# The second layer's gate path moved into its projections, and two of its decay tables behind them

## The chip, the cores and the metric

The kernel runs on one core of one Trainium2 chip. The metric is the device time of one execution in microseconds, taken as the median of several runs. A core has TensorE (matmuls into eight banks of PSUM), VectorE, ScalarE, GpSimd and SyncE; here SyncE only issues DMAs. In the profile they are PE (PEld: its weight loads), DVE, ACT, POOL and SP.

## What is computed

Two networks stand one behind the other; the change is in the second one ("second block"), in the last of its two layers. A layer mixes 256 latent tokens and 256 context tokens of width 1024 and then applies an MLP. The mixer projects all tokens, runs two kinds of linear attention in both directions, and projects back. In the last layer the context is only read: it gives keys, values and gates but gets no output.

```python
def gla_log_gate(d, up, ub):
    return jax.nn.log_sigmoid((d @ up + ub).astype(jnp.float32)) / GLA_GATE_NORM

def hybrid_mixer(h, hc, w_in, ret_decay, gate_up, gate_b, gla_norm_g, row_pos, col_pos, need_ctx):
    lat = project_in(h, w_in)
    cx = project_in(hc, w_in)
    log_gamma = jnp.log1p(-jnp.exp(ret_decay.astype(jnp.float32)))
    ...
    r_lat, r_ctx = bidirectional_scan(retention_inputs(lat, True), retention_inputs(cx, False))
    g_lat, g_ctx = bidirectional_scan(gla_inputs(lat), gla_inputs(cx))
```

"Retention" has four heads of 128 with one constant decay for each head and direction. The "gated half" has four heads of 64 keys and 128 values, whose decay comes from the data: two rank-16 projections (`parts[8]`, `parts[9]`), a product with `gate_up`, a log-sigmoid, and a running sum over each chunk, from which exponentials are taken.

## The kernel before, in words

Matmuls that carry much weight are done as three products of high and low halves (`mm3`, L569): a value is split into a rounded high half and a remainder. The small ones of the attention are plain fp32. In the profile nearly all matmuls stand on L561, transposes on L576.

**Loads and splits.** SyncE streams weight chunks of 2 MB into a ring of four slots (`load`, L295). In the projections of the second block a chunk of 512 columns uses two numbers: the raw chunk lies in slot n, VectorE writes its high half into slot n+1 and its low half over the raw one (`split_chunk`, L2365: a cast on L2369, a subtraction on L2370). The ring therefore holds two such chunks. A load waits for `used`, a counter that TensorE raises with the first plain matmul after a chunk is done (`chunk_used`, L588, and `mm`, L560), or, where `flush` (L580) stands, with a drain.

**Projections of layer 1.** TensorE goes through chunks 0 to 6 in order and then a small eighth one with the 32 rank columns (the "rank tile"). A chunk has four tiles, taken round four banks (`tile_bank`, L592); ScalarE evicts each (`take`, L1398). Chunks 0 (retention queries), 3 and 6 (the output gates of the two halves) and the first two tiles of chunk 4 (gated queries) are needed for the latent tokens only, so they are 256 columns wide ("narrow"); chunks 1, 2, 5 (keys, values) and the rest of chunk 4 (gated keys) are 512 wide. Behind chunk 2 the rotations of queries and keys run (fp32, into banks 4 to 7), which VectorE applies behind its split of chunk 4. GpSimd computes the arguments of the decay tables of all four retention heads (`head_args`, L1892; lines 1896 to 1902), ScalarE their exponentials behind chunk 6 (`head_exps`, L1641). In layer 0 only heads 0 and 1 are done there and the other two in the attention, because their place is in use.

**Phase end.** `phase_end` (L538) is a barrier of four engines: each drains, raises `phase` and waits for all (PEq, ACTq or DVEq on L540 in the profile).

**Attention.** TensorE runs the four retention heads; for each head: a state product, scores, an intra product and an inter product, then two transposes for the next head. The eight matmuls of the gate products stand between the first scores and the first state. ScalarE copies transposed keys and states (`keys_out`, `state_out`), takes gates out with their bias (`gate_out`, L1696) and computes the log-sigmoid's logarithm in three steps (`gate_soft`, L1702). VectorE scales values and applies decay (`head_prep`, `head_decay`, `head_norm`), and for the gated half does a subtraction and two scans for a direction (`gate_sums`, L2473), then arguments, products, masks and states. Every engine's order is written out by hand; no scheduler reorders it. Behind it come the output projection and the MLP.

Of the kernel before, what the change touches and what calls it, by code (L numbers as in the profile page):

```python
# [19 lines left out]
F32 = mybir.dt.float32  # L20
F32R = mybir.dt.float32r
# [130 lines left out]
def build(nc, T, out):  # L152
    ctx = ExitStack()
    with ctx:
# [21 lines left out]
        mrow = [sb("mod_rows", [P, 512])[:, :], RS[:, :]]  # L176
        et = sb("chunk_decay", [P, 64])
        AR = 25600
        with ExitStack() as once:
# [6 lines left out]
            ar = shared("arena", [P, AR])  # L186

# [3 lines left out]
        ar_r = sb("arena_r", [P, AR], F32R)  # L191
        ps = [ctx.enter_context(nc.psum_tensor(f"bank{b}", [P, 512], F32))[:, :] for b in range(8)]
# [28 lines left out]
        MLP1 = L1 + 18  # L221
        END = MLP1 + 16
        WIN_ORDER = [1, 0, 3, 2, 4, 5, 6, 7, 8, 9, 10, 11]
# [70 lines left out]
        def _(sp):  # L294
# [60 lines left out]
            for l, first, mlp in ((0, L0, MLP0), (1, L1, MLP1)):  # L355
                for j in range(7):
                    load(first + 2 * j, cols(T["w_in_2"][l], j * 512, 512), as_cols(first + 2 * j))
                load(first + 14, cols(T["w_in_2"][l], 7 * 512, 2 * RANK), as_cols(first + 14, 2 * RANK))
                for j in range(2):
                    load(first + 16 + j, cols(T["w_out_2"][l], j * 512, 512), as_cols(first + 16 + j))  # L360
# [127 lines left out]
        first_w, second_w = [A3(22944, 2, L), A3(23456, 2, L)], [halves(mrow[0]), halves(RS[:, :])]  # L488
        third_w = [[A3(18848, 2, L), A3(19360, 2, L)], [X[:, 0:2, L:2 * L], X[:, 2:4, L:2 * L]]]
        fourth_w = [[A3(19872, 2, L), A3(20384, 2, L)], [X[:, 4:6, L:2 * L], X[:, 6:8, L:2 * L]]]  # L490
        WD_RQD = [[first_w, second_w, third_w[l], fourth_w[l]] for l in range(LAYERS)]
# [7 lines left out]
        GT1 = [H[:, 2 * d:2 * d + 2, :] for d in range(2)]  # L499
        GLg = [H[:, 4 + 2 * d:6 + 2 * d, :] for d in range(2)]  # L500
        GQM, GQD = GT1, GLg
# [54 lines left out]
        def _(pe):  # L556
# [491 lines left out]
            for l, first, mlp in ((0, L0, MLP0), (1, L1, MLP1)):  # L1048
                W = 2 * L if l == 0 else L
                for j in range(7):  # L1050
                    n = first + 2 * j
                    chunk_in(n + 1)
                    wh, wl = as_cols(n + 1, slot=low), as_cols(n, slot=low)
# [17 lines left out]
                    elif j in (2, 5):  # L1071
# [6 lines left out]
                    else:  # L1078
                        for nt in range(4):
                            wide = 2 * L if j == 1 or (j == 4 and nt >= 2) else W  # L1080
# [6 lines left out]
                    if j == 2:  # L1087
                        flush()
                        pe.wait_ge(S("b2_in"), 16 * (4 + 2 * l))
# [7 lines left out]
                n = first + 14  # L1097
                chunk_in(n + 1)
# [254 lines left out]
        def _(act):  # L1353
# [281 lines left out]
            for l in range(LAYERS):  # L1635
# [14 lines left out]
                for j in range(8):  # L1650
# [1063 lines left out]
```

## Time and profile before

| | us |
|---|---|
| median of three runs (1963.90, 1963.91, 1969.85) | 1963.91 |
| the profiled execution | 1969.83 |
| its span | 1968.0 |
| TensorE busy | 1866.7 (95%) |
| VectorE busy | 817.0 (42%) |
| ScalarE busy | 585.8 (30%) |
| GpSimd busy | 389.1 (20%) |
| mean granted clock of TensorE | 0.983 |

The busy times are for the whole span. Matmuls are pipelined, so TensorE's 95% doesn't say that each of its microseconds is needed. The granted clock is a share of 2.4 GHz. In the rows further down, a timeline row is start, length, engine, line, operation, outputs from inputs and their shapes; brackets give the idle time before it and who ended it. Several instructions in a row without a gap are merged (x16). A full fp32 matmul stands as two records.

### The profile page before, as it was taken

Reading aid. Unit: us, or ns where it says so; the run is one execution under the profiler, and the core shown is the slowest. Engines: PE = TensorE matmul, PEld = TensorE weight load, DVE = VectorE, ACT = ScalarE, POOL = GpSimd, SP = SyncE. Lnnn points to the kernel's source line nnn. Section 1 sums busy time; section 2 is a strip of 40 time slices with the busy share of each in tenths; the row PEclk is TensorE's granted clock in tenths of the full one; section 3 lists DMA queues with packets and bytes.
Section 4 is the critical chain, followed back from the end, with each engine's and each line's share of the span. In section 5 each row is a group of like instructions: output and inputs, shape, how many; then the busy total and the mean of one; then the engine's idle time right before and its main releaser. Section 6 shows DMA issues by size and latency. Waiting matters only on the chain.

```text
span 1968.0 us, 26165 instructions
## 1 busy us (share of the span) xinstructions
PE 1866.7 (95%) x11248; PEld 1367.2 (69%) x11248; DVE 817.0 (42%) x1342; ACT 585.8 (30%) x892; POOL 389.1 (20%) x205
## 2 busy tenths in 40 slices
PE   5999999999998989989999899999999899889998
PEld 2777796964443443436887657888888688679998
DVE  1615244731110111115342844556665625574333
ACT  2513103331111111114112535222333411544554
POOL 2000000120000000006002131443343250025665
PEclk9999999989999999999999999999999899999999
DMA  9469917569999999992223104345444232414451
GB/s 357 154 255 347 339 44 278 199 257 420 427 427 427 428 427 428 426 417 91 95 86 123 41 33 154 140 177 187 156 150 150 87 113 102 174 51 164 173 197 38
DMA packets 111425, 429.84 MB, mean 218 GB/s; under 512 B 5706, under 2 KB 8821, under 8 KB 98512
## 3 DMA queue, kind: packets, MB, share of 16 engines
q1 hardware_dynamic: 109056, 416.56, 54.5%
q0 software_dynamic: 2256, 11.62, 1.6%
q8 instruction: 90, 1.47, 0.3%
q14 instruction: 23, 0.19, 0.0%
HBM read 427.11 MB, written 1.05 MB: 218 GB/s over the span
## 4 chain that ended last, share of the span: by engine, by line
PE 66%; DMA 17%; DVE 5%; PEld 5%; ACT 3%; issue 3%; PEldq 1%; SPq 0%; POOL 0%; POOLq 0%; ACTq 0%; DVEq 0%
PE bank L561 65%; DMA ring<-in_moe_w_down 7%; PEld bank L561 4%; DMA H<-in_moe_w_down 4%; DMA arena<-in_moe_w_down 4%; DMA ring<-in_ada_w 2%; PE bank L576 1%; PEldq L540 0%; DVE H L1985 0%; DMA ring<-in_w_in 0%; DVE arena L2508 0%; DVE H_low L1992 0%; DVE ring_low L2584 0%; DVE ring_low L2165 0%; DVE ring_low L2578 0%
## 5 line engine op out<-in xcount | busy, mean ns | idle before, releaser
L561 PE MATMUL bank<-arena_r 128*128 128x256 f32 (+1 forms) x2176 | 591.1, 339 | 12.4 <-ACT arena_r L1385 6.5
L561 PE MATMUL bank<-arena_r,ring_low 128*128 128x512 f32 (+2 forms) x1920 | 596.0, 342 | 1.5 <-DVE H_low L1992 1.0
L561 PEld LDWEIGHTS bank<-arena_r 128*128 128x128 f32 x2176 | 384.5, 190 | 63.6 <-issue 18.8
L561 PE MATMUL bank<-arena 128*128 128x64 bf16 (+8 forms) x2892 | 362.4, 318 | 40.4 <-DMA arena<-in_hy_filt_w 11.7
L561 PEld LDWEIGHTS bank<-arena_r,ring_low 128*128 128x128 f32 (+1 forms) x1920 | 352.3, 188 | 47.4 <-issue 2.5
L561 PEld LDWEIGHTS bank<-arena 128*128 128x128 bf16 (+4 forms) x2892 | 203.8, 131 | 200.1 <-issue 172.4
L561 PE MATMUL bank<-H_low,arena_r 128*128 128x512 f32 (+1 forms) x672 | 216.5, 339 | 0.0
L561 PE MATMUL bank<-ring,arena 128*64 128x512 f32 x768 | 170.3, 598 | 10.0 <-DMA ring<-in_moe_w_down 9.5
L2566 DVE SCALAR_TENSOR_TENSOR X<-bank,mod,X 128x256 f32<-128x256 f32 x216 | 94.2, 478 | 196.6 <-PE bank L561 196.6
L1924 POOL TENSOR_TENSOR ring_low<-ring,arena_r 128x2048 fp32r<-128x2048 f32 x31 | 142.4, 4615 | 130.5 <-DVE ring_low L2578 68.6
L1399 ACT ACTIVATE arena<-bank 128x512 f32<-128x512 f32 (+2 forms) x106 | 51.2, 496 | 366.3 <-PE bank L561 366.2
L2338 DVE SCALAR_TENSOR_TENSOR arena_r<-bank,arena,arena_r 128x512 fp32r<-128x512 f32 x32 | 24.0, 750 | 308.8 <-ACT arena_r L1582 308.8
L1940 POOL TENSOR_TENSOR arena_r<-arena,arena_r 128x512 fp32r<-128x512 f32 (+1 forms) x64 | 104.5, 1646 | 222.9 <-ACT arena L1802 222.9
L561 PEld LDWEIGHTS bank<-ring,arena 128*64 128x64 f32 x768 | 56.7, 138 | 116.4 <-issue 116.1
L561 PEld LDWEIGHTS bank<-H_low,arena_r 128*128 128x128 f32 x672 | 125.0, 191 | 14.4
L2634 DVE SCALAR_TENSOR_TENSOR arena<-ring,arena 128x1024 f32<-128x1024 f32 x84 | 99.5, 1222 | 66.1 <-POOL arena_r L1940 62.6
L561 PE MATMUL bank<-H,arena 128*64 128x512 f32 (+4 forms) x464 | 116.3, 433 | 6.7 <-DVE arena L2508 2.5
L561 PE MATMUL bank<-X,ring 128*128 128x256 f32 x512 | 118.1, 386 | 0.0
L561 PEld LDWEIGHTS bank<-X,ring 128*128 128x128 f32 x512 | 96.5, 192 | 17.8 <-issue 4.7
L1795 ACT ACTIVATE arena_r<-ring 128x4096 fp32r<-128x4096 f32 x15 | 54.5, 3630 | 172.8 <-DMA ring<-in_w_mlp 123.8
L561 PE MATMUL bank<-H_low,ring_low 128*128 128x512 f32 (+2 forms) x272 | 93.4, 358 | 0.0
L561 PE MATMUL bank<-ring_low,arena_r 128*128 128x512 f32 x288 | 92.8, 394 | 0.0
(326 smaller groups left out, 1854.0 us busy)
## 6 DMA issues: line engine op xcount, KB each, us to landing
ring<-in_w_mlp SPq DMA_DIRECT2D x32, 2048.0 KB, 7.9
ring<-in_w_in SPq DMA_DIRECT2D x26, 2048.0 KB, 8.9
ring<-in_ada_w SPq DMA_DIRECT2D x24, 2048.0 KB, 11.7
ring<-in_moe_w_up SPq DMA_DIRECT2D x17, 2048.0 KB, 23.0
ring<-in_moe_w_gate SPq DMA_DIRECT2D x17, 2048.0 KB, 27.5
arena<-in_moe_w_up SPq DMA_DIRECT2D x15, 2048.0 KB, 22.7
ring<-in_moe_w_down SPq DMA_DIRECT2D x14, 2048.0 KB, 23.4
arena<-in_moe_w_down SPq DMA_DIRECT2D x13, 2048.0 KB, 24.2
```

Source lines behind the costliest of these rows:

```text
L561: ins = nc.tensor.matmul(o, l, r, start=start, stop=stop, skip_group_check=True)
L576: ins = nc.tensor.transpose(o, i, ident)
L1399: A_(o, i, f, **kw).then_inc(S("tile_free"), 1)
L1795: A_(W2h, slot(n), ACT.Copy).then_inc(S("w_high"), 1)
L1924: G.tensor_tensor(low(n)[:, s], slot(n)[:, s], W1h[:, s].bitcast(F32), ALU.subtract).then_inc(S("w1_split"), 1)
L1940: G.tensor_tensor(HAl[:, nt, 0:W], HA[:, nt, 0:W], HAh[:, nt, 0:W].bitcast(F32), ALU.subtract)\
L2338: V.scalar_tensor_tensor(YSl[:, s], ps[6 + nb][:, :], WSL, YSh[:, s].bitcast(F32), ALU.mult, ALU.subtract)\
L2566: i = V.scalar_tensor_tensor(X[:, t, s * L:(s + 1) * L], o[:, s * L:(s + 1) * L], mod[:, 1 + l, gate + t, s:s + 1], X[:, t, s * L:(s + 1) ...
L2634: d = V.scalar_tensor_tensor(CPROD[:, c, :], as_turned(n)[:, q % 3, :], 1.0, CSIL[:, c, :], ALU.mult, ALU.mult, accum_out=mod[:, 2, bass.d ...
```

## The change

In layer 1 alone:

- The chunks come in the order 0, 1, 2, 3, 6, 4, 5 (`IN_ORDER`). The eighth chunk is gone; `w_out` and the MLP's chunks move up by two numbers.
- The 32 rank columns come by a DMA of GpSimd into `mod_rows` (`TINY`), issued behind that of the gate weights, ahead of the end of layer 0's MLP. VectorE splits them ahead of chunk 2. TensorE does the rank tile right behind the rotations, ahead of chunk 3.
- The gate products stand ahead of the tiles of the sixth chunk in order (chunk 4), into banks 4 to 7. ScalarE takes them out and computes the first direction's logarithm behind chunk 6, the second one's ahead of the last chunk's tiles. VectorE does the first direction's running sums behind the last split, the second's behind the arguments of the column decays, the last thing ahead of the phase end; each as four scans of 256 in place of two of 512.
- The buffers of gates and logarithms move to places free in layer 1 (parts of `YT`, `RQ` and `X`). The decay tables of heads 2 and 3 take the places that they have in layer 0, and so are computed behind the phase end; head 1's table moves to `X`.

In layer 0 only views are written differently. Two semaphores are merged into one (`small_exp`).

```diff
@@ loads
+        IN_ORDER = ((0, 1, 2, 3, 4, 5, 6), (0, 1, 2, 3, 6, 4, 5))
+        OUT_AT = (16, 14)
-                for j in range(7):
-                    load(first + 2 * j, cols(T["w_in_2"][l], j * 512, 512), as_cols(first + 2 * j))
-                load(first + 14, cols(T["w_in_2"][l], 7 * 512, 2 * RANK), as_cols(first + 14, 2 * RANK))
+                for j, c in enumerate(IN_ORDER[l]):
+                    load(first + 2 * j, cols(T["w_in_2"][l], c * 512, 512), as_cols(first + 2 * j))
+                if l == 0:
+                    load(first + 14, cols(T["w_in_2"][l], 7 * 512, 2 * RANK), as_cols(first + 14, 2 * RANK))
@@ places
-        third_w = [[A3(18848, 2, L), A3(19360, 2, L)], [X[:, 0:2, L:2 * L], X[:, 2:4, L:2 * L]]]
-        fourth_w = [[A3(19872, 2, L), A3(20384, 2, L)], [X[:, 4:6, L:2 * L], X[:, 6:8, L:2 * L]]]
+        first_w, third_w, fourth_w = [[A3(o, 2, L), A3(o + 512, 2, L)] for o in (22944, 18848, 19872)]
+        second_w = [[halves(mrow[0]), halves(RS[:, :])], [X[:, 0:2, L:2 * L], X[:, 2:4, L:2 * L]]]
@@ TensorE, projections
+                def gate_mms(banks):
+                    for d in range(2):
+                        for t in range(2):
+                            mm(ps[banks[2 * d + t]], GUP[0:32, d, t * P:(t + 1) * P], DT[0:32, :], inc="gate_mm")
+                for j, chunk in enumerate(IN_ORDER[l]):
                     n = first + 2 * j
                     chunk_in(n + 1)
+                    if l and j == 5:
+                        pe.wait_ge(S("tile_free"), gates_tile + 1)
+                        gate_mms((4, 5, 6, 7))
...
+                        if l:
+                            pe.wait_ge(S("ranks_split"), 1)
+                            gates_tile = tiles[0]
+                            ranks_tile(*[t.rearrange("p (k n) -> p k n", k=KT) for t in (TINYh, TINY_r)])
@@ ScalarE
-                for j in range(8):
+                for j in (0, 1, 2, 3, 4, 5, 6, 7) if l == 0 else (0, 1, 2, 7, 3, 6, 4, 5):
+                    if l and j == 5:
+                        gate_soft(1)
...
                     if j == 6:
                         tables()
-                        for h in range(2 + 2 * l):
+                        for h in range(2):
                             head_exps(h)
+                        if l:
+                            for d in range(2):
+                                gate_out(d)
+                            gate_soft(0)
...
                 head_square(0)
-                if l == 0:
-                    head_exps(2)
+                head_exps(2)
                 state_out(1)
@@ GpSimd
                 if l:
+                    pool.wait_ge(S("ada_turned"), 8)
+                    bring(TINY.rearrange("p (k n) -> p k n", k=KT), cols(T["w_in_2"][l], 7 * 512, 2 * RANK), "b2_in")
                     phase_end(pool, "l0_mlp")
...
-                for h in range(1, 2 + 2 * l):
-                    head_args(h)
+                head_args(1)
                 phase_end(pool, f"l{l}_in")
-                for h in range(2 + 2 * l, RT_H):
+                for h in range(2, RT_H):
                     head_args(h)
@@ VectorE
+                if l:
+                    dve.wait_ge(S("b2_in"), 16 * (4 + 3 * l))
+                    link(V.tensor_copy(TINYh, TINY))
+                    V.tensor_tensor(TINY_r, TINY, TINYh.bitcast(F32), ALU.subtract).then_inc(S("ranks_split"), 1)
                 for j in range(1 + l, 5):
                     split_chunk(first + 2 * j)
...
+                if l:
+                    gate_sums(0)
...
                 i.then_inc(S("col_arg"), 1)
+                if l:
+                    gate_sums(1)
                 phase_end(dve, f"l{l}_in")
```

## Rows read from the trace of the kernel before

**Rows 1.** The page, part 4: the chain that ended last, shares of the span.

```profile
PE 66%; DMA 17%; DVE 5%; PEld 5%; ACT 3%; issue 3%; PEldq 1%; SPq 0%; POOL 0%; POOLq 0%; ACTq 0%; DVEq 0%
```

**Rows 2.** The chain in order of time, 1618 to 1692: start, length, what.

```profile
1618.72 15.18 PE bank L561 x112
...
1634.32 50.87 PE bank L561 x288
...
1688.06 0.52 ACT mod_rows L1644
...
1691.85 0.33 PE bank L576
```

**Rows 3.** Table by stretches: length, each engine's busy us, granted clock, DMA share, GB/s.

```profile
1690.80:1738.90 48.10, 37.39 (x264) 30.17 (x264) 37.00 (x68) 27.47 (x48) 3.61 (x2) 0.93 0.39 146
```

**Rows 4.** Timeline of ScalarE: start, length, what; two of the gate evictions.

```profile
1694.24 0.69 ACT L1699 ACTIVATE H<-bank,vecs 128x512 f32<-128x512 f32 x1 [1.47 <-PE bank L561]
1695.10 0.69 ACT L1699 ACTIVATE H<-bank,vecs 128x512 f32<-128x512 f32 x1 [0.17 <-PE bank L561]
```

**Rows 5.** Timeline of VectorE, the same attention: sums of one direction, last retention norm.

```profile
1701.53 1.22 DVE L2475 SCALAR_TENSOR_TENSOR H<-H 128x1024 f32<-128x1024 f32 x1 [2.08 <-ACT H L1706]
1702.79 2.34 DVE L2480 TENSOR_TENSOR_SCAN H<-arena,H 128x512 f32<-128x512 f32 x2
...
1724.32 0.42 DVE L2468 TENSOR_TENSOR arena<-arena 128x256 f32<-128x256 f32 x1
```

**Rows 6.** All DMAs of GpSimd's line: length min/median/max, first and last start.

```profile
L1833 POOL DMA_DIRECT2D arena<-in_wr x1: 899/899/899, 364.4 to 364.4; - x1
```

**Rows 7.** Table by stretches, while the rank tile runs.

```profile
1685.20:1690.70 5.50, 5.50 (x24) 2.38 (x22) 0.00 (x0) 5.46 (x10) 0.00 (x0) 1.00 0.77 251
```

**Rows 8.** Timeline of SyncE's queue: issues of two loads in the projections.

```profile
1634.71 0.37 SPq L301 DMA_DIRECT2D ring<-in_w_in  x1
...
1651.58 0.37 SPq L301 DMA_DIRECT2D ring<-in_w_in  x1
```

**Rows 9.** Timeline of VectorE in the projections: splits, with idle time and releaser.

```profile
1629.80 4.42 DVE L2370 TENSOR_TENSOR ring_low<-ring,ring_low 128x4096 fp32r<-128x4096 f32 x1
...
1643.84 2.29 DVE L2369 CAST ring_low<-ring 128x4096 fp32r<-128x4096 f32 x1 [2.06 <-DMA ring<-in_w_in]
...
1659.36 2.29 DVE L2369 CAST ring_low<-ring 128x4096 fp32r<-128x4096 f32 x1 [8.69 <-DMA ring<-in_w_in]
```

**Rows 10.** Timeline of ScalarE: evictions of two narrow tiles in a row.

```profile
1631.05 0.39 ACT L1399 ACTIVATE arena<-bank 128x256 f32<-128x256 f32 x1 [2.49 <-PE bank L561]
1633.93 0.38 ACT L1399 ACTIVATE arena<-bank 128x256 f32<-128x256 f32 x1 [2.49 <-PE bank L561]
```

**Rows 11.** Table by stretches of 2 us around a wait of TensorE.

```profile
1769.00:1771.00 2.00, 0.28 (x2) 0.00 (x0) 1.37 (x1) 0.54 (x2) 0.00 (x0) 1.00 0.54 137
1771.00:1773.00 2.00, 0.37 (x3) 0.40 (x4) 1.36 (x4) 1.26 (x3) 0.00 (x0) 1.00 1.01 397
1773.00:1775.00 2.00, 2.00 (x14) 2.00 (x14) 2.00 (x6) 1.02 (x2) 0.00 (x0) 0.67 1.01 416
1775.00:1777.00 2.00, 2.00 (x11) 2.00 (x11) 2.00 (x6) 1.42 (x3) 0.00 (x0) 0.50 0.27 107
```

**Rows 12.** GpSimd: tables in layer 0's attention, in layer 1, starts of line 1896.

```profile
1071.71 1.67 POOL L1896 TENSOR_SCALAR arena<-arena 128x512 f32<-128x512 f32 x1 [136.63 <-ACTq L540]
...
1084.21 1.44 POOL L1902 TENSOR_SCALAR arena<-arena 128x256 f32<-128x256 f32 x1
...
1607.54 5.13 POOL L1899 TENSOR_TENSOR mod_rows<-mod_rows,RS 128x512 f32<-128x512 f32 x1
...
1715.48 1.81 POOL L1914 MEMSET arena<- 128x2048 f32 x1 [88.14 <-PE bank L561]
...
L1896 POOL TENSOR_SCALAR mod_rows<-arena x2: 1566/1567/1568, 928.7 to 1602.6; 128x512 f32<-128x512 f32 x2
L1896 POOL TENSOR_SCALAR X<-arena x2: 1566/1569/1572, 1614.6 to 1620.9; 128x512 f32<-128x512 f32 x2
```

More of the change, by code:

```diff
@@ L497, in build, with four, by_chunk @@
         RMU = et[:, 48:64]
-        GT1 = [H[:, 2 * d:2 * d + 2, :] for d in range(2)]
-        GLg = [H[:, 4 + 2 * d:6 + 2 * d, :] for d in range(2)]
-        GQM, GQD = GT1, GLg
+        def four(a):
+            return a.rearrange("p t (s n) -> p (t s) n", s=2)
+        GT1 = [four(H[:, 2 * d:2 * d + 2, :]) for d in range(2)]
+        GRAW = (GT1, [YT[:, 0:4, L:2 * L], RQ[:, 0:4, L:2 * L]])
+        GLG_OF = ([four(H[:, 4 + 2 * d:6 + 2 * d, :]) for d in range(2)], [YT[:, 4:8, L:2 * L], X[:, 4:8, L:2 * L]])
+        GQM = GT1
+        TINY, TINY_r, TINYh = mrow[0][:, 0:KT * 32], mrow_r[:, 0:KT * 32], mrow_r[:, KT * 32:2 * KT * 32]
+        def by_chunk(l, a):
+            return a.rearrange("p q (c k) -> p (q c) k", k=P) if l == 0 else a.rearrange("p q (c k) -> p q c k", k=P)
         GKE = [A3(0, 2, 512), A3(4096, 2, 512)]
@@ L1070, in _ @@
                                    "tile_done" if k == KT - 1 else None)
-                    elif j in (2, 5):
+                    elif chunk in (2, 5):
                         for tb in range(4):
@@ L1079, in _ @@
                         for nt in range(4):
-                            wide = 2 * L if j == 1 or (j == 4 and nt >= 2) else W
+                            wide = 2 * L if chunk == 1 or (chunk == 4 and nt >= 2) else W
                             o = tile_bank()
@@ L1127, in _ @@
                     scores(0, side)
-                for d in range(2):
-                    for t in range(2):
-                        mm(ps[(5, 1, 2, 3)[2 * d + t]], GUP[0:32, d, t * P:(t + 1) * P], DT[0:32, :], inc="gate_mm")
+                if l == 0:
+                    gate_mms((5, 1, 2, 3))
                 for h in range(RT_H):
@@ L1250, in _ @@
                 g_sum(1)
-                chunk_in(first + 16)
+                chunk_in(first + OUT_AT[l])
                 out_tile(0, (0, 1))
@@ L2426, in _, with each, gate_sums @@
                     split_chunk(first + 2 * j)
-                split_chunk(first + 14, KT * 2 * RANK)
+                if l == 0:
+                    split_chunk(first + 14, KT * 2 * RANK)
+                GLg = GLG_OF[l]
+                def each(e):
+                    return bc(e, [P, 8, P]) if l == 0 else bc(e, [P, 4, 2, P])
+                def gate_sums(d):
+                    dve.wait_ge(S("g_soft"), 2 * l + d + 1)
+                    link(V.scalar_tensor_tensor(GLg[d], GRAW[l][d], 0.0, GLg[d], ALU.min, ALU.subtract))
+                    for lg in [H[:, 4 + 2 * d + t, :] for t in range(2)] if l == 0 else [GLg[d][:, q, :] for q in range(4)]:
+                        r = R128[d][:, 0:2 * L // (l + 1)]
+                        if d:
+                            lg, r = lg[:, ::-1], r[:, ::-1]
+                        i = V.tensor_tensor_scan(lg, r, lg, 0.0, ALU.mult, ALU.add)
+                    link(i)
+                if l:
+                    gate_sums(0)
                 dve.wait_ge(S("tile_free"), 48 + 29 * l + 12)
@@ L2568, in add @@
                     return i
-                n = first + 17
+                n = first + OUT_AT[l] + 1
                 dve.wait_ge(full[n % RING], arrived(n))
```

127 lines of the change are left out of this document (65 added, 62 removed).

## The prediction

> **What bounds the kernel now.** I read the page first, then the chain of waits, then the second block's layer 1 stage by stage. The page's chain puts two thirds of the span on TensorE [rows 1]: an edit helps only where TensorE waits, or where it shortens what TensorE does. Two stretches of layer 1 matter. From 1573.7 to 1690.7 us the projections run; the chain there is TensorE work with one hole, between 1633.90 and 1634.32 [rows 2]. From 1691.85, TensorE's first transpose [rows 2], to 1738.9 us the attention runs; the table by stretches shows TensorE and VectorE busy for 37 us each out of 48 [rows 3]. No engine is full there: a relay of VectorE, ScalarE and TensorE decides. The change takes work out of the second stretch and puts it into the first, so the question is what the first charges for it.
>
> **Projections: what is hidden.** The logarithms of the gates (three ScalarE operations over 1024 columns for one direction) and the running sums (VectorE 1.22 + 2.34 us for one direction, [rows 5]) run beside TensorE. In the projections TensorE needs ScalarE only for evicting tiles and VectorE for splitting weights. ScalarE's burst behind chunk 6 (a table load, four exponentials 0.52 apart [rows 2], four gate evictions, one logarithm) ends some 10 us after that chunk; chunk 4's four tiles have four banks of their own, so nobody waits for it. VectorE's sums stand behind the last split in its order. Both count as zero; the cover would be gone, at 3.6 us a direction, only if a sum stood ahead of a split, and none does.
>
> **The weights of the gate ranks.** They come no longer as an eighth chunk but by one GpSimd DMA behind the gate weights, at about 1550 us. The nearest row is that of the router weights, short runs too: 0.90 us of issuing [rows 6]. Behind it on GpSimd stands the phase end of the layer before, which TensorE reaches only after its sums of squares. Bounds 0 and 0.9 us; I take 0, as TensorE is the later one by about 4 us. The split of these weights (128x256) stands on VectorE ahead of a wait for a load and costs nothing. The rank tile itself takes TensorE 5.5 us [rows 7] in either place.
>
> **The gate products** are four matmul pairs in full fp32, 0.86 us each by the distance of two evictions that follow them [rows 4]: 3.44 us. They now stand between chunk 6 and chunk 4, where TensorE is the bound: +3.44 us. Their removal is counted with the attention.
>
> **A new stall, the main term.** The ring holds two chunks. The load of number j starts when the first matmul of number j-1 has run and so released j-2. In the trace TensorE resumes at 1634.32 [rows 2], the next load is issued at 1634.71 [rows 8], and VectorE begins its split at 1643.84; a split is 2.29 + 4.42 us and 0.1 between [rows 9]. For the following number it is 1651.58 and 1659.36. So from the first matmul of one chunk until the next can be used: 0.39 + 9.13 + 6.8 + 0.1 = 16.4 us in the one case, 0.39 + 7.78 + 6.9 = 15.1 us in the other. A chunk must last as long to cover it. Chunk 4 does (one issue to the next, 16.9 us, [rows 8]). A narrow chunk, four tiles 2.88 us apart [rows 10], lasts 11.5. Before, the narrow chunk 3 had the rotations ahead of it (15.2 us together [rows 2]) and left a hole of 0.43; the narrow chunk 6 was followed only by the small rank weights. The new order 0, 1, 2, 3, 6, 4, 5 puts chunk 6 alone in front of a full chunk: TensorE waits 3.6 to 4.9 us, I take 4.2. The old hole closes, since the rank tile's 5.5 us now lie in front of chunk 3. Next comes chunk 5's load: it is released only behind the gate products, and chunk 4 covers it, by 0.5 us at the least.
>
> **The clock behind the stall.** A wait of this length has a price of its own in this trace. Around 1769 to 1773 us TensorE stood for about 3.3 us; the granted clock of the stretches behind is 0.67 and 0.50 [rows 11], the lower level (1.2 GHz) for some 3.3 us, each costing half of itself where TensorE is the bound: 1.7 us. Bounds 0 and 3.4 us (twice as long). I take 1.7, the row nearest in length.
>
> Projections: 4.2 - 0.43 + 3.44 + 1.7 = **+8.9 us**.
>
> **Attention: the relay without its logarithms and sums.** Out go 3.44 us of TensorE, four evictions and six wide operations of ScalarE, 7.1 us of VectorE. In come, behind the phase start T, two decay tables on GpSimd and their four exponentials. I followed each engine's order by hand from T (1691.85 before, TensorE's first transpose). GpSimd's bound is new. Its nearest rows are layer 0's, which does just this: two tables from 1071.71 to 1085.65, 7.0 us each [rows 12]. So the arguments of head 3 are there at T+14.0, its exponentials, two at 0.52 [rows 2], at T+15.1. Behind them in ScalarE's order stands the state of head 2, so TensorE ends head 2 at T+16.3 and head 3 (copies of 0.4, products of 0.9 us) at T+20.4. Before, head 3 was done at T+23.6, when the clearing that waits for it starts [rows 12]: 3.2 us gained. From there ScalarE's exponentials of the first direction and two inverse roots, and VectorE's products and masks, lead to the last retention norm. VectorE passed through the second direction's sums there (3.6 us); that is saved, but 1.8 us of it turn into a wait for ScalarE. The norm ended at 1724.74 [rows 5], T+32.9; now T+27.9. All behind it is unchanged VectorE work without a hole. Gain **-5.0 us**. Bounds: with tables of 6.3 us, the distance of the last two starts of layer 1 (1614.6 and 1620.9 [rows 12]), 1.5 us more, -6.5; with each a microsecond slower than in layer 0, -3.
>
> One rule bears on this term. In layer 1's second table, 12.0 us long against 6.3 for the last two, a GpSimd product took 5.13 us; it overlapped a VectorE product of the kind that takes 4.42 [rows 9, 12]. The Trainium skill, "SBUF — State Buffer", section "Who interferes with whom", says that a VectorE product with both inputs in SBUF keeps out a GpSimd operation that reads SBUF until it ends. By that rule the trace's 5.13 us is a wait, and rival A is what it would do here.
>
> **Sum.** +8.9 - 5.0 = +3.9 us. The profiled execution took 1969.83 us (span 1968.0, 1.8 around it), which would become 1973.7. The median of the runs is 1963.91, with one of the three at 1969.85 like the profiled one. The edit is the same for either, so I put it on the median: 1967.8 us. Its own range from the bounds: 3.6 - 0.4 + 3.4 + 0 - 6.5 = +0.1 up to 4.9 - 0.4 + 3.4 + 3.4 - 3.0 = +8.3.
>
> **Rivals.** A, slower: a decay table in the attention collides with VectorE. Place: the second of the two, beside the wide arguments of the gates. Price: a table as long as the one of layer 1 that began at 1602.6 and ended at 1614.6 (12.0 us, [rows 12]) instead of 7.0, +5 us, the whole gain; +8.9, 1972.8 us. It decides from 2 us of extra time on. Against it: layer 0 has the same order and shows 7.0. Chance 0.12.
> B, the stall is hidden because loads land faster: -0.43 + 3.44 - 5.0 = -2.0, 1961.9 us. Against it: the gate products stand behind the wait for the chunk, and even the faster landing leaves 3.6 us. Chance 0.07.
> C, the change doesn't bring what it says: VectorE's order and not its work decides, each removed sum turns into a wait for ScalarE; gain 1, sum +7.9, 1971.8 us. For it: 1.8 of 3.6 us go that way already. Chance 0.08.
> D, the same +3.9, but the median lies with the upper of the two values seen (1969.85), 1973.7 us. For it: one of three runs and the profiled one. Chance 0.23.
> The forecast has 0.46; 0.04 is left for anything else.
>
> **Numbers.** Time 1967.8, range 1961.5 (B) to 1974.5 (D and its surroundings). A measurement of this kernel can tell about 0.3% (5.9 us) from no change. Faster needs more than B: 0.04. Slower: A, C and D, 0.43, less 0.08 for those that stay under the bound, plus 0.05 of the forecast's upper end: 0.40. Same: 0.56.
>
> **What would show it.** Right: an idle time of TensorE of 3.6 to 4.9 us at about 1651 us, put down to VectorE's split; a granted clock near 0.5 behind it; the attention's first transposes near 1700.7 instead of 1691.85; the last retention norm 28 us after them instead of 33; GpSimd's two tables 14 us long. Wrong: no idle time there; an attention shorter by under 3 us or over 7; a GpSimd operation of 3 us or more among its tables; the phase end before layer 1 waiting for GpSimd.

## The result

The changed kernel takes 1976.25 us (median of 7 runs), the kernel before 1968.02 us (7 runs beside it; 1968.2 to 1968.6 over the 26 to 33 runs that stand beside each group of experiments). The ratio is 1.004, 95% interval 1.0023 to 1.0057: some 8 us slower, where +3.9 was predicted. The profiled executions stand 11.3 us apart (spans 1979.3 and 1968.0). 3.0 us of that lie ahead of layer 1's first projection, in work that the change doesn't touch (that point falls between 1567.6 and 1578.5 us over all profiles here, whichever kernel it is). 8.3 us lie in the two stretches of the prediction:

| stretch of layer 1 | before | after | predicted change | measured |
|---|---|---|---|---|
| projections: first projection to the first transpose, T | 118.12 us | 127.53 us | +8.9 | +9.4 |
| attention: T to the first sum of the gated outputs | 47.27 us | 46.14 us | -5.0 | -1.1 |
| behind it, to the MLP's first matmul | 33.51 us | 33.51 us | 0 | 0 |

TensorE's timeline around the new order's weak place; the columns are start, length, engine, line, operation, and in brackets the idle time before it with what ended it:

```profile
1653.69 0.28 PE L576 MATMUL bank<-arena_r,ring_low 128*128 128x256 f32 x1
1657.29 5.39 PE L576 MATMUL bank<-arena 32*128 32x512 f32 x8 [3.31 <-DVE ring_low L2416]
1662.60 0.58 PE L576 MATMUL bank<-arena_r,ring_low 128*128 128x256 f32 x1
```

Chunk 6 ends, TensorE stands for 3.31 us until VectorE's split, and then the gate products (32 of 128 rows, "32x512") take 5.39 us instead of 3.4. VectorE's timeline shows the load landing at 1650.41, 7.80 us after its issue, and the split behind it, as in [rows 9]:

```profile
1642.61 20.98 SPq L304 DMA_DIRECT2D ring<-in_w_in  x2
...
1650.41 2.29 DVE L2415 CAST ring_low<-ring 128x4096 fp32r<-128x4096 f32 x1 [5.57 <-DMA ring<-in_w_in]
1652.81 4.42 DVE L2416 TENSOR_TENSOR ring_low<-ring,ring_low 128x4096 fp32r<-128x4096 f32 x1
```

The table by stretches (behind the stretch its length, then each engine's busy time; the third number from the right is the granted clock):

```profile
1654.00:1657.00 3.00, 0.00 (x0) 0.00 (x0) 3.00 (x1) 2.96 (x5) 0.00 (x0) 1.00 0.01 3
1657.00:1659.00 2.00, 1.72 (x4) 0.85 (x5) 0.23 (x1) 1.45 (x3) 0.00 (x0) 1.00 0.00 0
1659.00:1660.00 1.00, 1.00 (x3) 0.38 (x2) 0.00 (x0) 0.82 (x2) 0.00 (x0) 0.57 0.00 0
1660.00:1665.00 5.00, 5.00 (x15) 2.98 (x14) 0.00 (x0) 2.94 (x4) 0.00 (x0) 0.50 0.12 15
1665.00:1666.00 1.00, 1.00 (x7) 1.00 (x7) 0.00 (x0) 0.97 (x2) 0.00 (x0) 0.51 0.92 344
```

From 1659.1 to 1666 us TensorE is busy at the lower level (1.2 GHz): 6.8 us, twice the stretch of [rows 11], so about twice its price.

In the attention, GpSimd's two tables, the waits on ScalarE and TensorE behind them, and the two marks that the prediction named (GpSimd's clearing that waits for head 3, the last retention norm):

```profile
1711.45 1.56 POOL L1943 TENSOR_SCALAR arena<-arena 128x512 f32<-128x512 f32 x1
1712.99 1.82 POOL L1944 TENSOR_SCALAR arena<-arena 128x512 f32<-128x512 f32 x1
1714.89 1.27 POOL L1946 TENSOR_TENSOR arena<-arena 128x512 f32<-128x512 f32 x1
1716.26 0.93 POOL L1948 TENSOR_SCALAR arena<-arena 128x256 f32<-128x256 f32 x1
1717.16 2.90 POOL L1949 TENSOR_SCALAR arena<-arena 128x256 f32<-128x256 f32 x1
1728.87 1.81 POOL L1960 MEMSET arena<- 128x2048 f32 x1 [8.81 <-PE bank L576]
...
1716.93 1.21 DVE L2546 TENSOR_TENSOR H<-arena 128x1024 f32<-128x1024 f32 x1
1718.07 1.21 DVE L2547 TENSOR_TENSOR arena<-arena 128x1024 f32<-128x1024 f32 x1
...
1720.09 0.63 ACT L1677 ACTIVATE arena<-arena 128x512 f32<-128x512 f32 x1 [3.78 <-POOL arena L1949]
...
1721.56 2.07 PE L576 MATMUL bank<-arena 128*128 128x256 f32 x4 [3.55 <-ACT arena L1740]
...
1735.16 0.43 DVE L2539 TENSOR_TENSOR arena<-arena 128x256 f32<-128x256 f32 x1
```

The tables run from 1704.32 to 1720.06, 15.7 us instead of 14.0. The last product of the second takes 2.90 us (0.93 for its like); 2.1 of them it runs beside VectorE's two wide products. TensorE stands 3.55 us for what follows from it, and again finds a low clock behind the wait. In the next fence, of the same kernel, the lower level covers most of the 8 us from 1720:

```profile
1704.28:1719.00 14.72, 12.53 (x68) 10.20 (x68) 10.06 (x22) 4.40 (x11) 14.32 (x10) 1.00 0.76 285
1720.00:1728.00 8.00, 6.44 (x22) 5.37 (x23) 3.18 (x7) 5.13 (x10) 0.06 (x1) 0.57 0.00 0
```

### The profile page after: what moved, and what is told of

Its sections match the earlier page's. It is cut to its first block, busy times and chain, and to the rows that moved or that the text cites. A ratio compares the mean times of both kernels' runs of the same rounds, so it can differ in the third digit from the quotient of the medians.

```text
span 1979.3 us, 26170 instructions
## 1 busy us (share of the span) xinstructions
PE 1877.4 (95%) x11248; PEld 1375.6 (69%) x11248; DVE 819.2 (41%) x1346; ACT 586.6 (30%) x892; POOL 394.0 (20%) x206
## 4 chain that ended last, share of the span: by engine, by line
PE 65%; DMA 17%; DVE 5%; PEld 5%; issue 3%; ACT 2%; SPq 2%; POOL 1%; PEldq 0%; DVEq 0%; ACTq 0%
PE bank L576 64%; DMA ring<-in_moe_w_down 7%; PEld bank L576 4%; DMA H<-in_moe_w_down 4%; DMA arena<-in_moe_w_down 4%; DMA ring<-in_w_in 2%; SPq L304 1%; PE bank L591 1%; PEldq L555 0%; DVE H L2031 0%; DVE arena L2572 0%; DVE H_low L2038 0%; DVE ring_low L2650 0%; DVE ring_low L2211 0%; DVE ring_low L2416 0%
## 5 line engine op out<-in xcount | busy, mean ns | idle before, releaser
L576 PE MATMUL bank<-arena_r 128*128 128x256 f32 (+1 forms) x2176 | 591.7, 339 | 11.3 <-ACT arena_r L1418 6.5
L576 PE MATMUL bank<-arena_r,ring_low 128*128 128x512 f32 (+1 forms) x1904 | 592.5, 342 | 1.1 <-DVE H_low L2038 1.0
L576 PE MATMUL bank<-arena 128*128 128x64 bf16 (+8 forms) x2916 | 370.3, 319 | 45.6 <-DMA arena<-in_hy_filt_w 11.6
L576 PEld LDWEIGHTS bank<-arena_r,ring_low 128*128 128x128 f32 x1904 | 352.3, 190 | 46.5 <-issue 3.4
L576 PEld LDWEIGHTS bank<-arena 128*128 128x128 bf16 (+4 forms) x2916 | 210.5, 133 | 204.9 <-issue 168.8
L1970 POOL TENSOR_TENSOR ring_low<-ring,arena_r 128x2048 fp32r<-128x2048 f32 x31 | 142.4, 4617 | 130.4 <-DVE ring_low L2644 68.2
## 6 DMA issues: line engine op xcount, KB each, us to landing
ring<-in_moe_w_down SPq DMA_DIRECT2D x14, 2048.0 KB, 23.3
```

The lines of the kernel that those rows point to most:

```text
L576: ins = nc.tensor.matmul(o, l, r, start=start, stop=stop, skip_group_check=True)
L1970: G.tensor_tensor(low(n)[:, s], slot(n)[:, s], W1h[:, s].bitcast(F32), ALU.subtract).then_inc(S("w1_split"), 1)
```

## The experiments

All times are against the kernel before, measured on the same chip beside them (medians 1968.2 to 1968.6). The stretches are read from TensorE's timeline of each kernel's one profiled execution.

| kernel | median us | ratio, 95% interval | projections | attention |
|---|---|---|---|---|
| before | 1968.02 | | 118.12 | 47.27 |
| changed | 1976.25 | 1.0040 (1.0023 to 1.0057) | 127.53 | 46.14 |
| order only | 1976.53 | 1.0038 (1.0024 to 1.0051) | 124.15 | 50.64 |
| gate products in the wait | 1967.80 | 1.0002 (0.9990 to 1.0015) | 120.99 | 45.87 |
| dummy matmuls in the wait | 1972.50 | 1.0024 (1.0012 to 1.0037) | 125.85 | 46.05 |
| ranks behind chunk 3 | 1967.93 | 0.9996 (0.9981 to 1.0010) | 120.94 | 46.02 |
| gate products over 128 rows | 1972.42 | 1.0017 (1.0000 to 1.0033) | 125.85 | 48.19 |
| fourfold products, 32 rows | 1990.83 | 1.0114 (1.0090 to 1.0137) | 141.18 | 46.13 |
| fourfold products, 128 rows | 1976.25 | 1.0043 (1.0023 to 1.0062) | 130.89 | 45.90 |
| tables early | 1971.06 | 1.0019 (0.9999 to 1.0039) | 129.19 | 40.96 |
| two more GpSimd products | 1977.14 | 1.0042 (1.0021 to 1.0063) | 127.60 | 48.93 |
| products in the wait, tables early | 1967.05 | 0.9985 (0.9969 to 1.0001) | 122.49 | 42.46 |
| ranks behind chunk 3, tables early | 1967.81 | 0.9989 (0.9971 to 1.0006) | 122.50 | 41.96 |
| the same, products over 128 rows | 1964.56 | 0.9981 (0.9966 to 0.9997) | 122.18 | 41.32 |

**The order alone.** Edit, on the kernel before; the gate products, logarithms and sums stay in the attention:

```diff
-                for j in range(7):
+                for j, chunk in enumerate(IN_ORDER[l]):   # layer 1: 0, 1, 2, 3, 6, 4, 5
```

> The kernel before with one edit: layer 1's chunks in the order 0, 1, 2, 3, 6, 4, 5 and the rank chunk last; gates, sums and decay tables stay in their old places. Theory (the order itself makes the stall): TensorE waits 3.3 to 4.9 us ahead of chunk 4, with the granted clock at its lower level behind it for 1.7 to 3.4 us of extra time; the hole of 0.43 us ahead of the narrow chunk stays; projections from 118.1 us to 123 to 126 us, attention unchanged at 47 us; the whole +5 to +8 us against before. Rival (the stall needs the gate products or the sums beside it): no wait over 1 us, the whole within 1 us of before.

```profile
1649.50 0.39 PE L562 MATMUL bank<-arena_r,ring_low 128*128 128x256 f32 x1 [4.59 <-issue]
...
1650.00:1653.00 3.00, 3.00 (x16) 3.00 (x16) 0.00 (x0) 0.92 (x2) 0.00 (x0) 0.50 0.62 164
1701.00:1707.00 6.00, 6.00 (x17) 4.23 (x16) 0.69 (x1) 2.60 (x4) 0.00 (x0) 0.50 1.05 386
```

TensorE stands 4.59 us, without any other part of the change (the view puts it down to "issue"; it ends 0.10 us behind VectorE's split, 1644.98 and 4.42 long). Behind it the clock is low for 3.4 us. So the wait belongs to the order. The order costs as much as the whole change, though I expected its attention to stay as it was: 50.64 us instead of 47.27. It holds another low clock, 6.8 us long, which starts 2.9 us into the gate products (they run from 1697.96 to 1702.29) and has no wait ahead of it but the phase end. That was the first sign that the wait is not the only thing that lowers the clock.

**The gate products into the wait.** They need only the rank tile, so they can go ahead of the wait for chunk 4's weights:

```diff
-                    chunk_in(n + 1)
                     if l and j == 5:
+                        pe.wait_ge(S("rotated"), 2)
                         pe.wait_ge(S("tile_free"), gates_tile + 1)
                         gate_mms((4, 5, 6, 7))
+                    chunk_in(n + 1)
...
+                    if m:
+                        dve.drain().then_inc(S("rotated"), 1)
```

> The changed kernel with the gate products ahead of the wait for chunk 4 in place of behind it (and a signal from VectorE that the rotations have been read, so that the banks are free). Theory (stall, clock and gate products add up in the projections): the products fill the wait of 3.3 us, no idle time over 1 us is left there, the granted clock stays at 1, the products are 0.86 us each in place of 1.71; projections from 127.5 to about 121 us, the whole 6.4 us less than the changed kernel, about +2 against before. Rival (the extra time lies ahead of layer 1 or in its attention): the whole as the changed kernel, +8 against before.

```profile
1640.00:1665.00 25.00, 25.00 (x157) 21.28 (x156) 10.54 (x4) 11.24 (x18) 0.00 (x0) 1.00 0.40 144
```

No idle time and a clock of 1.00 throughout: projections 120.99 us, 6.5 less than the changed kernel, and the whole level with the kernel before. That is the stall's 3.3 us and the clock's 3.1, both gone.

**Dummy matmuls in the wait.** 14 matmuls of 512 columns, whose result nobody reads, keep TensorE busy until the weights are there (VectorE's signal `rotated` is the one of the last edit):

```diff
+                    if l and j == 5:
+                        pe.wait_ge(S("rotated"), 2)
+                        for i in range(14):
+                            nc.tensor.matmul(ps[4], Hh[:, 0, 0:P], Hh[:, i % KT, :], start=True, stop=True, skip_group_check=True)
                     chunk_in(n + 1)
```

> The changed kernel with 14 matmuls of 512 columns more, of no use, that run in TensorE's wait for chunk 4 (3.2 us of work in 3.3 us of wait). The work that counts starts no earlier. Theory (the clock is a cost of its own): the granted clock stays at 1 behind the wait, the gate products are 0.86 us each in place of 1.71, projections 127.5 to about 124.4 us, the whole 3 us less than the changed kernel, +5 against before. Rival (the low clock in that place costs nothing, or has other causes): the time of the changed kernel, +8.

```profile
1644.76 3.36 PE L1085 MATMUL bank<-arena_r 128*128 128x512 f32 x14
1648.24 3.72 PE L576 MATMUL bank<-arena 32*128 32x512 f32 x8
1651.88 0.58 PE L576 MATMUL bank<-arena_r,ring_low 128*128 128x256 f32 x1
...
1648.00:1651.00 3.00, 2.88 (x8) 1.30 (x8) 0.18 (x1) 2.22 (x4) 0.00 (x0) 1.00 0.02 5
1651.00:1652.00 1.00, 1.00 (x4) 0.22 (x2) 0.00 (x0) 0.70 (x2) 0.00 (x0) 0.89 0.00 0
1652.00:1655.00 3.00, 3.00 (x14) 3.00 (x15) 0.00 (x0) 2.94 (x4) 0.00 (x0) 0.50 0.41 91
```

The gate products now run at the full clock, but behind them it still falls for 3.4 us, with TensorE never idle. Only half of the low clock went with the wait. That the rest comes from the gate products was a guess at this point, since the kernel with the products in the wait has them too and shows no low clock. It gave theory K: matmuls over a quarter of the rows bring the granted clock down behind them.

**The rank tile behind chunk 3.** The other way to take the wait away, by what stands between two loads:

```diff
-                        if l:
-                            pe.wait_ge(S("ranks_split"), 1)
-                            gates_tile = tiles[0]
-                            ranks_tile(*[t.rearrange("p (k n) -> p k n", k=KT) for t in (TINYh, TINY_r)])
+                    if l and j == 3:
+                        pe.wait_ge(S("ranks_split"), 1)
+                        gates_tile = tiles[0]
+                        ranks_tile(*[t.rearrange("p (k n) -> p k n", k=KT) for t in (TINYh, TINY_r)])
...
-                for j in (0, 1, 2, 3, 4, 5, 6, 7) if l == 0 else (0, 1, 2, 7, 3, 6, 4, 5):
+                for j in (0, 1, 2, 3, 4, 5, 6, 7) if l == 0 else (0, 1, 2, 3, 7, 6, 4, 5):
```

> The changed kernel with one thing different: the rank tile stands behind chunk 3 instead of in front of it, so the order is 0, 1, 2, 3, ranks, 6, 4, 5. Then two narrow chunks and the rank tile (17 us) lie between the release of a ring buffer and chunk 4's need. Theory (the wait is only a matter of what stands between two loads): the wait of 3.3 us at 1654 is gone, the old one of about 0.4 us ahead of a narrow chunk comes back, and with the wait goes the lower clock behind it; projections 121.6 to 123.3 us instead of 127.5, the whole 4 to 6 us under the changed kernel, so within 2.5 us of the kernel before. If the gate products themselves bring the clock down, wherever they stand, 1.7 to 3 us of that are not gained: projections 124 to 125. Rival (loads land late for another reason): a wait of over 2 us stays.

```profile
1637.54 2.29 DVE L2415 CAST ring_low<-ring 128x4096 fp32r<-128x4096 f32 x1 [1.41 <-DMA ring<-in_w_in]
1639.94 4.43 DVE L2416 TENSOR_TENSOR ring_low<-ring,ring_low 128x4096 fp32r<-128x4096 f32 x1
...
1645.02 3.69 PE L576 MATMUL bank<-arena 32*128 32x512 f32 x8
```

Chunk 4's split is done at 1644.37, before chunk 6 ends at 1645.0. No idle time at all (the old hole of 0.4 that I expected back is missing too), no low clock: 120.94 us, lower than the 121.6 I gave as the least. The whole is 1967.93, level with the kernel before.

**The gate products over all rows.** The 96 rows that were unused are cleared once, so the sums, columns and instructions stay the same:

```diff
+            G.memset(A(14336, 1024), 0.0).then_inc(S("rows_clear"), 1)
...
-                            mm(ps[banks[2 * d + t]], GUP[0:32, d, t * P:(t + 1) * P], DT[0:32, :], inc="gate_mm")
+                            mm(ps[banks[2 * d + t]], GUP[:, d, t * P:(t + 1) * P], DT[:, :], inc="gate_mm")
```

> The changed kernel, with the gate products of both layers and both directions taken over all 128 rows of their operands instead of 32 (the other 96 rows are cleared once at the start, so the sums are the same and the columns and their number too). Theory K (matmuls that use a quarter of the rows bring the granted clock down behind them, as behind the dummy matmuls' run without an idle time): the low clock behind the wait in the projections, some 7 us of it, is shorter or gone, projections 1.7 to 3.1 us shorter, and layer 0's low clock behind its gate products at about 1077 us goes too; the whole 1.7 to 4 us under the changed kernel. Rival (it is the idle time of 3.3 us alone that lowers the clock): projections 127 to 128 and layer 0 unchanged, the whole within 1 us of the changed kernel.

```profile
1648.13 4.38 PE L576 MATMUL bank<-arena 128*128 128x512 f32 x6 [3.26 <-DVE ring_low L2418]
...
1649.00:1653.00 4.00, 4.00 (x8) 1.61 (x6) 0.00 (x0) 1.83 (x3) 0.00 (x0) 0.57 0.00 0
1653.00:1665.00 12.00, 12.00 (x76) 10.71 (x75) 2.29 (x1) 4.92 (x8) 0.00 (x0) 1.00 0.50 176
```

The wait is there (3.26 us), but the low clock behind it is 3.4 us, not 6.8; projections 125.85, 1.7 less. As K has it. The attention takes 48.19 us and holds 13.7 us of low clock in three stretches (10.2 us in two in the changed kernel); single profiles can't tell that from chance. The pair that follows leaves no such doubt.

**The twins.** On the kernel with the rank tile behind chunk 3, so without a wait, layer 1's gate products are computed four times in a row, once over 32 rows and once over 128 (the second as in the last edit, with layer 0's products over 128 rows too):

```diff
+                            for again in range(4 if l else 1):
+                                mm(ps[banks[2 * d + t]], GUP[0:32, d, t * P:(t + 1) * P], DT[0:32, :], inc="gate_mm" if again == (3 if l else 0) else None)
```

> The run with the rank tile behind chunk 3 (no wait in front of chunk 4, so the idle time is out of the picture), with layer 1's gate products computed four times in a row, over 32 of 128 rows as before: 13.8 us of such products instead of 3.4, work added whose result is the same. At the full clock the projections take 120.9 + 10.3 = 131.3 us. Theory K (matmuls over a quarter of the rows bring the granted clock down, without an idle time): a low clock appears during and behind them, 3.4 to 10 us long or more, and the projections take 133 to 141 us. Rival (idle time alone does it): the clock stays at 1.00 and the projections take 131 to 132 us.

> The same with the fourfold gate products taken over all 128 rows (96 of them cleared to zero): the same columns, instructions and length at the full clock. Theory K (the rows count): the clock stays at 1.00, projections 131 to 132 us, 2 us or more under the twin over 32 rows. If it is only the kind of matmul (fp32, few columns at a time) and not the rows, both twins show the same low clock; if only the idle time counts, both show none.

First the twin over 32 rows, then, behind the dots in the middle, the twin over 128; 32 such matmuls each, of which the trace holds 28 and 26:

```profile
1648.25 20.25 PE L576 MATMUL bank<-arena 32*128 32x512 f32 x28
...
1652.00:1653.00 1.00, 1.00 (x3) 0.37 (x2) 0.00 (x0) 0.00 (x0) 0.00 (x0) 0.56 1.06 414
1653.00:1664.00 11.00, 11.00 (x14) 4.27 (x13) 6.72 (x2) 1.37 (x2) 0.00 (x0) 0.50 0.19 71
1664.00:1672.00 8.00, 8.00 (x19) 4.38 (x18) 0.00 (x0) 2.58 (x3) 0.00 (x0) 0.50 0.00 0
1672.00:1673.00 1.00, 1.00 (x8) 1.00 (x8) 0.00 (x0) 0.97 (x2) 0.00 (x0) 0.70 0.00 0
```

```profile
1648.20 11.32 PE L576 MATMUL bank<-arena 128*128 128x512 f32 x26
...
1652.00:1653.00 1.00, 1.00 (x4) 0.46 (x3) 0.00 (x0) 0.31 (x1) 0.00 (x0) 1.00 1.04 403
1653.00:1664.00 11.00, 11.00 (x55) 7.41 (x54) 7.20 (x3) 5.20 (x7) 0.00 (x0) 1.00 0.07 23
1664.00:1672.00 8.00, 8.00 (x42) 6.75 (x40) 7.90 (x9) 0.98 (x2) 0.00 (x0) 1.00 0.00 0
```

In both, TensorE is busy for all of these 20 us. Over 32 rows the clock falls 4 us after the products begin and comes back 4 us after they end, 20.5 us later; over 128 rows it stays at 1.00. Projections 141.18 against 130.89 (131.3 was worked out for the full clock). The medians are 14.6 us apart; what adds to the 10.3 us of the projections isn't shown in full. The rival, that only idle time lowers the clock, is refuted, and the twin of equal kind and columns rules out that it is fp32 or the number of instructions.

**The tables early.** The decay tables of heads 2 and 3 of layer 1 are computed during the projections, in buffers free by then, and ScalarE's exponentials of them stand behind chunk 6, so GpSimd has none left in the attention (of the edit, GpSimd's part):

```diff
-                head_args(1)
+                for h in range(1, 2 + 2 * l):
+                    if h == 3:
+                        pool.wait_ge(S("tile_done"), 48 + 29 + 13)
+                    head_args(h)
                 phase_end(pool, f"l{l}_in")
-                for h in range(2, RT_H):
+                for h in range(2 + 2 * l, RT_H):
```

> The changed kernel with the decay tables of heads 2 and 3 of layer 1 computed in the projections, as before the change, in other free memory. Theory (GpSimd's tables bound the attention and so ate the gain): projections unchanged at 127.5 us, attention from 46 to about 41 us, no wait over 2 us among the retention heads and no low clock there; the whole 5 us less than the changed kernel, +3 against before. Rival C (VectorE's order decides): attention 45 to 46 us, the whole +8 against before.

```profile
1720.51 2.00 PE L577 MATMUL bank<-arena 128*128 128x128 f32 x12 [1.24 <-DVE mod_rows L2531]
...
1730.58 0.43 DVE L2545 TENSOR_TENSOR arena<-arena 128x256 f32<-128x256 f32 x1
```

The attention takes 40.96 us, 5.2 less: the wait of 3.55 is gone, the longest left ahead of the last retention norm is 1.84. That norm ends at T+26.6 (1731.01 less 1704.37), where the changed kernel has T+31.3. The projections still hold the wait (3.27 us) and here even 10.2 us of low clock: 129.19.

**GpSimd made later.** Two more products of the tables' kind stand ahead of head 2's table:

```diff
+                    if l and h == 2:
+                        w = WD_RQD[l][h][0]
+                        for i in range(2):
+                            G.tensor_scalar(w, EF, lgam[:, h:h + 1], None, ALU.mult).then_inc(S("again"), 1)
+                            pool.wait_ge(S("again"), i + 1)
```

> The changed kernel with two extra GpSimd products (1.55 us each, 3.1 us in all, their results are overwritten) at the start of the attention of layer 1, ahead of head 2's decay table. Theory A (GpSimd's two tables set the end of head 3): TensorE's second wait for the state, 3.5 us at 1718, becomes some 3 us longer and the attention goes from 46.1 to about 49, the whole +2.5 to +4 us over the changed kernel. Rival C (the order of VectorE's work decides and GpSimd has slack): attention 46 to 46.5, the whole within 1 us of the changed kernel.

```profile
1698.26 3.46 POOL L1961 TENSOR_SCALAR arena<-arena 128x512 f32<-128x512 f32 x2 [87.09 <-ACTq L555]
...
1714.07 3.05 POOL L1949 TENSOR_SCALAR arena<-arena 128x256 f32<-128x256 f32 x1
...
1709.89 1.13 PE L576 MATMUL bank<-X,arena 128*128 128x256 f32 x4 [2.38 <-ACT arena L1740]
1718.62 1.13 PE L576 MATMUL bank<-arena 128*128 128x256 f32 x4 [2.67 <-ACT arena L1740]
```

3.46 us on GpSimd make the attention 2.8 us longer (48.93), with waits for the tables at both heads. The tables set the pace. The whole is only 0.9 us over the changed kernel in the medians, within their intervals; the stage alone shows it. (The last product is slow here as well, 3.05 us.)

**Both cures.** First the gate products in the wait with the tables early, then the rank tile behind chunk 3 with the tables early, then the latter with the gate products of both layers over 128 rows. The edits are those above; with the rank tile later, GpSimd's wait count is 17 instead of 13.

> The two earlier edits together: the gate products stand ahead of the wait for chunk 4's weights (as in the run that put them into the wait) and the decay tables of heads 2 and 3 of layer 1 are computed during the projections (as in the run with early tables). Theory (two independent losses: the wait with its clock, and GpSimd's tables in the attention): projections 120.5 to 122 us, attention 41 to 42.5, so 2.5 to 4.5 us under the kernel before, ratio about 0.998. Rival (the attention's gain with early tables came only because the projections were slower and the engines behind them had caught up): attention 44 or more, no gain over the kernel before.

> The changed kernel with the rank tile behind chunk 3 and the decay tables of heads 2 and 3 of layer 1 computed during the projections: no wait in front of chunk 4 and no GpSimd tables in the attention. Each alone has shown its stage: projections 120.9 us, attention 41.0 to 42.5 us. Theory (they are independent): both together, so 120.9 - 118.1 + 41.5 - 47.3 = 3.0 us under the kernel before, ratio about 0.9985. Rival (the early tables get in VectorE's way: in the runs with them the GpSimd products took 3.2 and 4.9 us beside VectorE's splits, and here fewer spare microseconds stand in front of chunk 4): a wait of over 1 us comes back in the projections, ratio 1.000 or more.

> The last one with the gate products of both layers over all 128 rows (96 cleared). Theory K: the low clock behind the gate products in layer 0's attention and here and there in layer 1 is rarer; 0 to 3 us under its twin over 32 rows. Rival (rows don't count): the same time as the twin within 1 us.

All three show both gains together and no wait over 0.3 us in the projections, so the early tables don't get in VectorE's way where it counts. The projections are 1.2 to 1.5 us over the 120.9 of the kernels without early tables: each holds one low clock of 3.4 us, the first two behind the gate products, the third at 1572 us, at its first chunk, where no gate product is near. The third is the only one whose interval lies wholly below one: 1964.56 us, 0.9981 (0.9966 to 0.9997), 3.6 us under the kernel before and 11.7 under the changed one, which ran in another group. Against its twin over 32 rows the 3.2 us of the medians lie within what the intervals allow.

## Why the prediction was wrong

**The base.** The sum was put on a median of three runs, 1963.91; more runs put the same kernel at 1968.0 to 1968.6. Half of the miss of 8.5 us is this: 1968.02 + 3.9 would have been 1971.9. Rival D named it as a danger, at a chance of 0.23, although the profiled execution (1969.83) and one of the three stood above.

**The stall: right in place, cause and kind.** In size, 3.31 us lie 0.3 under the lower bound (predicted 3.6 to 4.9, taken 4.2): from the issue at 1642.61 the load took 7.80 us, as in the faster of the two cases of [rows 8, 9], and the split 6.82; from the issue to the end of chunk 6 it was 11.4 us (1653.97), so of the narrow chunk's 11.5 us only 0.1 had passed at the issue, where I had counted 0.39. The order alone shows 4.59. Rival B, a hidden stall, falls.

**The gate products: right** in what they cost at full clock: 120.99 us with them in the wait is 118.12 - 0.43 + 3.44 = 121.13 but for 0.1.

**The clock behind the stall: the mis-sized term.** 9.4 - 3.3 + 0.4 - 3.4 leaves 3.1 us for the clock, where 1.7 was taken and 3.4 was the upper bound. The step took "the row nearest in length" for a wait. A wait alone does cost that: 3.4 us at the lower level with the order alone (4.59 us idle) and with full rows (3.26 us idle). What I did not see is that the gate products behind the wait add a cause of their own. Low clock in the projections, summed by stretches of 1 us: wait and products over 32 rows 6.8, 6.8 and 10.2 us (changed kernel, two more GpSimd products, tables early); products over 32 rows without a wait 0, 0, 3.4, 3.4 and 3.4 us; wait and 128 rows 3.4 us; 128 rows without a wait 0 and 3.4 us, the latter at the first chunk, 80 us ahead of the products. The trace of before held a hint that I passed over: in layer 0 the clock is low from about 1077.3 to 1080.8, right behind the attention's gate products (1073.77 to 1077.46), while TensorE has been busy since 1071.67:

```profile
1072.00:1077.00 5.00, 5.00 (x17) 2.68 (x16) 5.00 (x11) 1.76 (x3) 4.82 (x4) 1.00 1.05 388
1077.00:1081.00 4.00, 4.00 (x15) 3.31 (x14) 0.17 (x1) 1.46 (x3) 4.00 (x4) 0.57 1.05 389
```

**Hidden logarithms and sums: right.** ScalarE's first logarithm starts at 1663.30 and nobody waits; VectorE is idle for 12.9 us before the phase ends. The rank weights' new way cost nothing either: from the sums of squares to the first projection it is 23.3 us (24.3 before).

**The attention: wrong in size, 1.1 instead of 5.0 us** (under 3 us was one of the prediction's own signs of being wrong). The step that failed is the length of GpSimd's tables, "T+14.0", from layer 0's rows. It is T+15.8; head 3's exponentials end at T+17.0 instead of 15.1. That is rival A, the table colliding with VectorE's wide products, at a third of its price (1.8 us, not 5), though the rival put its threshold at 2 us. The Trainium skill, "SBUF — State Buffer", section "Who interferes with whom", says that a VectorE instruction with two SBUF inputs and a GpSimd instruction that reads SBUF exclude each other, and that the one issued first keeps the other out. The 2.90 and 3.05 us for an operation of 0.93 agree with it: in both kernels VectorE's first wide product had begun shortly before. No run here takes VectorE's products away from beside the tables, so this cause is read from the overlap alone. Of layer 0's rows I took the sum, 7.0 us a table; the same product, beside shorter VectorE work, stood there with 1.44 us [rows 12], the hint that it can be held off. The other half has no place in the prediction: TensorE's new wait of 3.55 us came with 6.8 us at the lower level. Six of the seven kernels with a wait of 3.54 to 3.56 us here show 6.8 us of it, one 3.4; the four whose gate products and tables both stand in the projections have neither this wait nor a low clock within T+22. The work from head 3's exponentials to its end took 7.6 us instead of 5.3 (T+17.0 to T+24.6). The one kernel with 3.4 us of low clock there (gate products over 128 rows) took 6.8 us for it, so by an estimate from these two the low clock accounts for some 1.7 of the 2.3 us; the rest is open. Together head 3 was done 4.2 us later than T+20.4. The last norm came 3.4 us late, at T+31.3 instead of 27.9, and what follows it took some 0.4 us more than before (why isn't shown). That makes up the 3.9 us that are missing. I had charged the clock for the stall in the first stretch and not for the wait that my own sum created in the second.

**Rival C**, that VectorE's order would keep the gain, falls: without GpSimd's tables the same order on VectorE gains 6.3 us (47.27 to 40.96).

In sum: in place and sign the three causes (stall, its clock, GpSimd as the new bound) were the right ones. The base was 4.1 us too low, the stall 0.9 too dear, the clock 1.4 too cheap, the attention 3.9 too good. That the measured change, +8.2 us by the medians, still lies just inside the sum's own range (up to +8.3) is luck: the attention lay outside its bounds, and the stall's lower price hid a part of it.

## What to carry to other kernels

A chunk's place in a ring is part of its cost: before moving work, compare for each load what stands between its release and its use with the load and split behind it; here moving a 5.5 us tile by one place was worth 6.6 us. Charge every new wait of TensorE of the length seen here (3.3 to 4.6 us), also one that your own plan creates, with a low clock behind it, and ask of short matmuls over few rows whether they can take all rows with zeros. A median of three runs is not a base for a sum of 4 us.

## What the runs showed of the hardware that I had not expected

- Matmuls over 32 of the 128 rows lower TensorE's granted clock though the engine is never idle: fourfold products over 32 rows ran at 0.50 for most of their length and the clock was low for 20.5 us, their twins over 128 rows, 96 of them zeros, at 1.00. The difference is 10.3 us in the projections of the two profiles and 14.6 us in the medians. The Trainium skill, "TensorE: Matmul & The Clock Gate", section "HAM oscillation — how this bites in real kernels", names idle time as what brings the clock down; the waits here agree (3.26 us idle, 3.4 us low), the twins show that it is not all.
- One short burst of such products (3.4 us) does it in some executions only: in layer 0 eight of eleven profiles with 32 rows show a low clock that begins 5.3 to 6.3 us after the attention's first transposes, and none of three with 128 rows.
- The stretches at the lower level in layer 1 measured 3.4, 6.8, 10.2 and 20.5 us in sum. The same unchanged code had more or fewer of them from one profile to the next: ahead of 1000 us, which is ahead of all that the change touches, 37.5 us in the profile of before and 68.2 us in that of the changed kernel.
- The last GpSimd product of a table, 128x256, took 2.90 and 3.05 us beside VectorE's two wide products, which read both inputs from SBUF, and 0.93 where VectorE did nothing beside it; in the trace of before, another product of 128x256, in layer 0's projections (at 922.82), took 4.97 us beside a split's subtraction.
